# Two-layer hybrid transformer block, one core: three FFN norms folded into the eviction, products of 384 and 386 columns

## What is computed

```python
def rms_norm(x, w):
    return x * lax.rsqrt(jnp.mean(x * x, axis=-1, keepdims=True) + NORM_EPS) * w

def modulate(h, shift, scale):
    return h * (1.0 + scale) + shift

def swiglu(h, w_in, w_out):
    gate, up = jnp.split(h @ w_in, 2, axis=-1)
    return (jax.nn.silu(gate) * up) @ w_out

for layer in range(2):
    h = h + 0.5 * lm[2] * swiglu(modulate(rms_norm(h, norm_w[layer, 0]), lm[0], lm[1]), ffn_w_in[layer, 0], ffn_w_out[layer, 0])
    ...
    h = h + lm[5] * y
    h = h + 0.5 * lm[8] * swiglu(modulate(rms_norm(h, norm_w[layer, 2]), lm[6], lm[7]), ffn_w_in[layer, 1], ffn_w_out[layer, 1])
```

## Time and profile before

| | |
|---|---|
| median of 3 runs | 2738.08 us (2736.44 to 2738.50) |
| the profiled execution, its own time | 2739.12 us |
| its span | 2737.2 us |
| PE (matmul) busy | 2664.7 us, 97% |
| DVE busy | 1521.2 us, 56% |
| ACT busy | 692.3 us, 25% |
| mean granted TensorE clock | 0.992 |
| chain that ended last, by engine | PE 91%, DVE 4%, ACT 2%, issue 1%, POOL 1% |

### The profile page before, as it was taken

How to read it: one execution, slowest core, us unless ns; L and a number is a source line. 1 busy time by engine, 2 the same in 40 slices (tenths; PEclk the granted TensorE clock), 3 DMA queues, 4 the chain that set the end, 5 groups by cost and what they waited for, 6 DMA issues and landing times.

```text
span 2737.2 us, 42267 instructions
## 1 busy us (share of the span) xinstructions
PE 2664.7 (97%) x15515; PEld 2290.5 (84%) x15515; DVE 1521.2 (56%) x2621; ACT 692.3 (25%) x1075; POOL 93.7 (3%) x211
## 2 busy tenths in 40 slices
PE   7999999999999999999999999999999989999998
PEld 4888888888877888888888888888887877888886
DVE  5776477534376477626763677247536465543333
ACT  4111111122256221111111311111113345422222
POOL 0000000000034000000000000000000022000000
PEclk8999999999999999999999999999999999999999
DMA  7877477412200177536762577257422200233332
GB/s 228 198 184 185 113 184 184 125 50 79 54 17 2 54 165 185 146 86 159 184 161 58 123 184 175 71 140 184 126 70 84 69 26 17 81 96 100 91 110 81
DMA packets 485795, 316.98 MB, mean 116 GB/s; under 512 B 30588, under 2 KB 483664, under 8 KB 485712
## 3 DMA queue, kind: packets, MB, share of 16 engines
q1 hardware_dynamic: 485712, 315.88, 45.2%
HBM read 313.73 MB, written 2.10 MB: 115 GB/s over the span
## 4 chain that ended last, share of the span: by engine, by line
PE 91%; DVE 4%; ACT 2%; issue 1%; POOL 1%; DMA 0%; SPq 0%; DVEq 0%; ACTq 0%; POOLq 0%
PE pg L709 79%; PE pg L776 4%; PE p L1047 1%; PE pn L1030 1%; PE pg L986 1%; PE p L724 1%; DVE xlo L1640 1%; DVE tnorm L1632 1%; PE pg L867 1%; ACT whi L1155 0%; DVE wlo L1493 0%; PE pg L991 0%; DVE probT L1847 0%; DVE mx L1854 0%; ACT xhi L1244 0%
## 5 line engine op out<-in xcount | busy, mean ns | idle before, releaser
L709 PE MATMUL pg<-xhi,whi 128*128 128x512 f32 (+1 forms) x2856 | 794.5, 347 | 4.1 <-DVE wlo L1493 4.0
L709 PE MATMUL pg<-xhi,wlo 128*128 128x512 f32 (+1 forms) x2856 | 788.6, 344 | 0.0
L709 PE MATMUL pg<-xlo,whi 128*128 128x512 f32 (+1 forms) x2856 | 787.1, 344 | 0.0
L1155 ACT CAST whi<-raw 128x1024 fp32r<-128x1024 f32 (+1 forms) x288 | 321.8, 1118 | 1060.2 <-PE pg L709 1045.9
L1493 DVE TENSOR_TENSOR wlo<-raw,whi 128x1024 fp32r<-128x1024 f32 (+1 forms) x288 | 377.6, 1311 | 350.5 <-ACT whi L1155 347.8
L709 PEld LDWEIGHTS pg<-xhi,whi 128*128 128x128 f32 x2856 | 451.3, 188 | 72.6 <-DVE wlo L1493 5.9
L709 PEld LDWEIGHTS pg<-xlo,whi 128*128 128x128 f32 x2856 | 450.4, 188 | 69.3
L709 PEld LDWEIGHTS pg<-xhi,wlo 128*128 128x128 f32 x2856 | 450.4, 188 | 68.9
L1577 DVE SCALAR_TENSOR_TENSOR part<-ada,cond,part 128x256 f32<-128x256 f32 x960 | 465.3, 485 | 32.7
L1703 DVE SCALAR_TENSOR_TENSOR h<-pg,gcol,h 128x512 f32 (+1 forms) x118 | 71.4, 639 | 442.3 <-PE pg L709 437.5
L709 PE MATMUL pg<-ahi,whi 128*128 128x512 f32 x1100 | 306.1, 346 | 0.0
(11 more groups left out here) (212 smaller groups left out, 1983.4 us busy)
## 6 DMA issues: line engine op xcount, KB each, us to landing
ada<-in_w_ada SPq DMA_DIRECT2D x512, 256.0 KB, 4.2
raw<-in_ffn_w_in SPq DMA_DIRECT2D x176, 512.0 KB, 3.9
raw<-in_ffn_w_out SPq DMA_DIRECT2D x64, 704.0 KB, 4.5
raw<-in_w_in SPq DMA_DIRECT2D x24, 512.0 KB, 3.8
ada_first<-in_w_ada SPq DMA_DIRECT2D x8, 1024.0 KB, 11.9
raw<-in_w_in SPq DMA_DIRECT2D x16, 256.0 KB, 3.5
raw<-in_w_o SPq DMA_DIRECT2D x16, 256.0 KB, 2.8
raw<-in_w_o SPq DMA_DIRECT2D x32, 128.0 KB, 2.9
```

The costliest lines, as they stand in the source:

```text
L709: last = nc.tensor.matmul(pg[s][:, p0:p1], w[:, s, k], v[:, k, p0:p1], start=(k == 0 and n == 0), stop=(k == kt - 1 and n == 2))
L1155: nc.scalar.copy(whi[:, s, 0:nk], raw[:, s, 0:nk]).then_inc(s_whi[s], 1)
```

## The change

It concerns the norms `m` = 0, 2 and 3 (`POST`), all of them ahead of an FFN over 768 tokens.

- **The operand.** `xhi`/`xlo` hold `h * acol` alone (norm weight and scale), without the root and without the shift. ACT makes `xhi` straight from `h` (`scaled_hi`) and DVE makes `xlo` straight from `h` (`scaled_low`). Two more columns, 768 and 769, hold the shift vectors of the latent and of the context tokens (`shift_columns_hi`, `shift_columns_low`), so rows of `xhi` and `xlo` are 776 floats apart instead of 768.
- **The products** of these phases go over columns 0 to 383 and 384 to 769, that is 384 and 386 columns, one to each bank of `pg[s]`.
- **The eviction.** DVE multiplies unit 0 by `rstd` from PSUM into `gate`, copies its two shift results to `gbias`, and frees PSUM. ACT then takes Silu from `gate` with `gbias` as bias, in two instructions. DVE multiplies unit 1 by `rstd` into `up`, and makes `(up + gbias) * gate` in two more.
- **The norm's order.** The root is taken behind the operands. In norm 3, the operands of `k` 0 to 5 are made ahead of the last pair's eviction (`EARLY_K`); in norm 2 all are made behind it.
- **The opening.** ACT squares the token rows of `xtok` with an accumulator into `ssq`, one number for each token; DVE spreads these on a diagonal, and the same matmul by ones turns it into a row. The eight squares and eight additions over `h` go. DVE copies five of the six transposes, ACT the last. PE's two sums of squares come ahead of the first modulation chunk. ACT loads the table and takes the roots behind the operands of the second chunk.

```diff
+        POST = (0, 2, 3)
+        EARLY_K = {3: KD - 2}
+        def product_parts(i, t):
+            if phases[i][0] in ("in", "win") and phases[i][2] in POST:
+                return [(0, TOK // 2, 0), (TOK // 2, XB, 512)]
+            return [(0, SEQ, 0)] + ([(SEQ, t, SEQ)] if t > SEQ else [])
...
-                parts = [(0, SEQ)] + ([(SEQ, TOK)] if t == TOK else [])
+                parts = product_parts(i, t)
...
-                        if part_ == 0 and (s, k) == (0, 1):
+                        if part_ == 0 and (s, k) == (order[-1] if m in POST else (0, 1)):
                             square_sums(m, 1)
             def opening_pair(i):
-                first_modulation(0)
                 square_sums(0, 0)
                 square_sums(0, 1)
+                first_modulation(0)
                 first_fold(0)
...
-            for tt in range(0, TOK // P, 2):
-                act.wait_ge(s_xT, tt + 1)
...
+            for tt in range(TOK // P):
+                act.wait_ge(s_x[tt // 2], 32)
...
+                nc.scalar.activation(sqjunk[tt % 2][:, :], xtok[:, tt, :], ACT.Square, accum_out=ssq[:, tt:tt + 1]
...
-            for k in range(KD):
-                square(0, k, k % 2, 1)
...
+            def scaled_hi(m, part_, k):
+                nc.scalar.activation(xhi[:, k, p0:p1], h[:, k, p0:p1], ACT.Identity, scale=acol[:, k, v:v + 1]
+                                     ).then_inc(s_xh, 1)
...
+                        if m in POST:
+                            split_hi(nxt, 0, jn)
+                            act.wait_ge(s_free[0], read_value(i, f))
+                            nc.scalar.activation(gate[:, 0:SEQ], gate[:, 0:SEQ], ACT.Silu, bias=gbias[:, 0:1])
+                            nc.scalar.activation(gate[:, SEQ:TOK], gate[:, SEQ:TOK], ACT.Silu, bias=gbias[:, 1:2]
+                                                 ).then_inc(s_gd, 1)
+                            split_hi(nxt, 1, jn)
+                            return
...
+            def scaled_low(m, part_, k):
+                nc.vector.scalar_tensor_tensor(xlo[:, k, p0:p1], h[:, k, p0:p1], acol[:, k, v:v + 1],
+                                               xhi[:, k, p0:p1].bitcast(f32), ALU.mult, ALU.subtract).then_inc(s_xn, 1)
...
+                        if m in POST:
+                            dve.wait_ge(s_unit[0], f + (j0 + 1))
+                            nc.vector.tensor_tensor(halves_of(gate[:, :]), unit_columns(0), halves_of(rstd[:, :]), ALU.mult)
+                            nc.vector.tensor_copy(gbias[:, 0:2], pg[0][:, shift_at]).then_inc(s_free[0], 1)
                         split_lo(nxt, 0, jn)
...
+                        if m in POST:
+                            nc.vector.tensor_copy(gbias[:, 2:4], pg[1][:, shift_at])
+                            nc.vector.tensor_tensor(halves_of(u), unit_columns(1), halves_of(rstd[:, :]), ALU.mult).then_inc(s_free[1], 1)
+                            dve.wait_ge(s_gd, gate_count(m, hf, f))
+                            for v, (p0, p1) in enumerate(((0, SEQ), (SEQ, TOK))):
+                                last = nc.vector.scalar_tensor_tensor(gate[:, p0:p1], u[:, p0:p1],
+                                                                      gbias[:, 2 + v:3 + v], gate[:, p0:p1],
+                                                                      ALU.add, ALU.mult)
```

More of the change, by code:

```diff
@@ L141, in transformer @@
         gate = place("gate", [P, TOK], f32, m0 + TOK * 4)
+        up = place("up", [P, HALF, TOK], f32, start["alo"])
+        gbias = sb("gbias", [P, 4])
+        sqjunk = [place(f"sqjunk{b}", [P, D], f32, at) for b, at in enumerate((m0 + 3 * TOK * 4, m0 + 4096))]
+        ssq = place("ssq", [P, TOK // P], f32, m0 + 3 * TOK * 4 + D * 4)
         xtok = place("xtok", [P, TOK // P, D], f32, start["alo"])
@@ L707, in split_product @@
                     for n, (w, v) in enumerate(((whi, hi), (whi, lo), (wlo, hi))):
-                        for p0, p1 in parts:
-                            last = nc.tensor.matmul(pg[s][:, p0:p1], w[:, s, k], v[:, k, p0:p1],
+                        for p0, p1, c0 in parts:
+                            last = nc.tensor.matmul(pg[s][:, c0:c0 + p1 - p0], w[:, s, k], v[:, k, p0:p1],
                                                     start=(k == 0 and n == 0), stop=(k == kt - 1 and n == 2))
@@ L1440, in _ @@
                     else:
-                        square_part(i, 0, 0)
-                        square_part(i, 0, 1)
+                        nn = next_norm(i)
+                        early = EARLY_K.get(nn, 0)
+                        if early:
+                            act.wait_ge(s_coef, coef_count(nn, 0))
+                            for part_ in range(2):
+                                if part_:
+                                    shift_columns_hi(nn, 0, KD)
+                                for k in range(early):
+                                    scaled_hi(nn, part_, k)
+                        for s in range(2):
+                            square_part(i, 0, s)
+                            if early:
+                                scaled_hi(nn, 0, early + s)
                 else:
@@ L1666, in norm @@
                         read_first(q)
-                        scaled(0, 2 * q)
-                        scaled(1, 2 * q)
-                        low(0, 2 * q)
-                        scaled(0, 2 * q + 1)
-                        low(1, 2 * q)
-                        scaled(1, 2 * q + 1)
+                        scaled_low(0, 0, 2 * q)
+                        shift_columns_low(0, 2 * q, 2 * q + 2)
+                        scaled_low(0, 1, 2 * q)
+                        scaled_low(0, 0, 2 * q + 1)
                         if q == 0:
                             copy_first(1)
-                        low(0, 2 * q + 1)
-                        low(1, 2 * q + 1)
+                        scaled_low(0, 1, 2 * q + 1)
+                    return
+                if m in POST:
+                    if phases[i][0] == "wo":
+                        for k in range(3):
+                            scaled_low(m, 0, k)
+                        add_part(i, 1, 0)
+                        split_lo(i + 1, 0, 0)
+                        scaled_low(m, 0, 3)
+                        sum_part(m, 1, 0)
+                        for k in (4, 5):
+                            scaled_low(m, 0, k)
+                        add_part(i, 1, 1)
+                        split_lo(i + 1, 1, 0)
+                        for k in (6, 7):
+                            scaled_low(m, 0, k)
+                        sum_part(m, 1, 1)
+                        shift_columns_low(m, 0, KD)
+                        for k in range(KD):
+                            scaled_low(m, 1, k)
+                    else:
+                        split_lo(i + 1, 0, 0)
+                        sum_part(m, 1, 0)
+                        add_part(i, 1, 1)
+                        scaled_low(m, 1, KD - 2)
+                        split_lo(i + 1, 1, 0)
+                        sum_part(m, 1, 1)
+                        scaled_low(m, 1, KD - 1)
                     return
@@ L1896, in step @@
                         dve.wait_ge(s_unit[1], f + (j0 + 1))
[L1897 removed]
+                        if m not in POST:
+                            dve.wait_ge(s_free[0], read_value(i, f))
                         col = slice(f, f + 1) if isinstance(f, int) else ds(f, 1)
@@ L1944, in _ @@
                         coefficients(nn)
+                        early = EARLY_K.get(nn, 0)
+                        for part_ in range(2):
+                            if early and part_:
+                                shift_columns_low(nn, 0, KD)
+                            for k in range(early):
+                                scaled_low(nn, part_, k)
                         for s in range(2):
@@ L1947, in _ @@
                             sum_part(nn, 0, s)
-                        add_part(i, 1, 0)
+                            if early:
+                                scaled_low(nn, 0, early + s)
+                        if early or nn not in POST:
+                            add_part(i, 1, 0)
                 else:
```

157 lines of the change are left out of this document (118 added, 39 removed).

## The result

| | before | after |
|---|---|---|
| median, same chip | 2738.29 us (2736.44 to 2741.03) | 2755.98 us (2753.76 to 2758.57) |
| ratio, 95% interval | | 1.0063 [1.0047, 1.0079] |
| the profiled execution, its own time | 2739.12 us | 2758.57 us |

A forecast was written before the change was run, and what follows sets the result against it. PE, busy 97% of the span, was taken to bound the kernel. Opening -4.5, norm 2 -3.5, norm 3 -4.0 and products +2.6 sum to -9.4 us: 2729 us, range 2721 to 2740.

The forecast's parts named there:

- the products' term: FFN products, 3168 couples: two more columns each, 0.83 ns, with the number of matmuls unchanged; +2.6 us.
- The rival of the slower pace: FFN products at the new widths run at the mixing's 355 ns a couple: 19.3 us more, 2748 us; chance 0.09.
- The lower end of the products' term: FFN products: a couple could fall to 770/2.4 + 2 x 8 ns, put at -15 us.
- the sign of being wrong: FFN loop: the prediction is wrong if a pair of units takes over 17.3 us, or PE's fold waits for DVE.
- Opening: Start to the first FFN's loop: earlier products, later third chunk, shorter operand waits and end; -4.5 us, ends -2.8 and -5.5.
- a wait ahead of the third fold: Opening: table load and roots delay the copy of chunk 2 beyond PE's other work; +1.0 us.
- Norm 2: Last pair to the FFN's loop: first product 2 us earlier, a later hole included; -3.5 us, ends -4.8 and -1.0.
- a hole of 1.40 us for 2.0 ahead of slot 1's products: Norm 2: slot 1's weights come late behind ACT's square and operands, so PE waits 2.0 us.
- The half of a low stretch: Norm 2: PE's clock may fall again, costing 1.7 to 3.4 us; half of the smaller was taken.
- Norm 3: Last pair to the FFN's loop: fewer waits, with six of eight operands made ahead; -4.0 us, ends -4.5 and -2.5.
- DVE's step: FFN loop's steady step: added DVE work disappears in a 2.69 us wait, margin 1.1 us; costed at nothing.
- the bound that it might stay low for 5 us of products: Opening's end of -2.8 us: clock at 0.50 rises at 39.6 only, so 5 us of products run at half rate.

The follow-up runs named there:

- the kernel without shift columns: The changed kernel with rows 768 floats apart, the two shift columns left out and products of 384 and 384 columns: 2722.54 us, ratio 0.9937.
- the rows above, of another kernel: The kernel before with the opening's part alone, squares from token rows and roots ahead of chunk 0's copy: 2740.04 us, ratio 0.9994.
- streams alone: Separate kernels that only stream the same matmuls, nothing else running, by row distance, widths, order and entry; 384 + 386 at 776 in the changed layout: 353 to 354 ns a couple.

## Why the prediction was wrong

**The step that failed** is the products' term: "a matmul costs its columns plus some 13.4 ns, whatever its width", hence +2.6 us. It measured 0.30 us a pair, +19.8 us over 66. The formula was fitted to 512 and 256, at a distance of 768, and used for 386 at 776. Half is the distance (16.90 with it alone), the rest two more columns and the split: at 832, where the distance is harmless, 384 + 386 still has 353 ns in every stretch. I had listed the change of row distance, under the rival, but as a matter of the 3168 couples. That the last FFN, with widths untouched, reads the same rows was not in the sum: +5.9.

**The rival of the slower pace** was nearest to what happened: it names the widths, the distance and the tail, and leaves open which counts. That its size fits, 6.1 ns a couple for 6.2, is partly luck: the 6.1 came from 512 + 256 at 768, and the 6.2 are a distance and a split. I gave it 0.09 because three streams fitted a formula. What should have weighed more is that the trace of before already held couples at 355 ns with no hole that I could name, and that its out phases, which I had not looked at one by one, don't all fit the formula. The stretch of 312 couples that holds the first out phase behind norm 2 (start, length, work), before:

```profile
1147.07 110.38 PE pg L709 x624
```

is 353.8 ns a couple, for the 346.8 of the formula. The rival's 2748 was short of 2756 by the last FFN's rows and the out phases' pace.

**Two slips beside it.** The lower end of the products' term does not follow from its working: 770/2.4 + 2 x 8 is 336.8 ns, 10 under the formula's 346.8 before, which is -32 us and not -15. And the sign of being wrong, a pair over 17.3 us, was set too far out: 17.05 was enough to lose 19 us.

**The out phases' pace** was missing too. Looking at six of them, not at one, would have shown two paces, and that 0.2% of the time can move by itself when code around a phase changes.

**What held.** Opening: -4.70 for -4.5; its first product at 34.88 for 34.5, with a wait ahead of the third fold of 0.36 us for 1.0. Norm 2: -4.6 for -3.5, with a hole of 1.40 us for 2.0 ahead of slot 1's products, and the clock did not fall behind it:

```profile
950.00:975.00 25.00, 23.60 (x147) 22.75 (x146) 16.08 (x28) 18.41 (x31) 0.00 (x0) 1.00 0.52 123
```

The half of a low stretch that I had charged was not paid. Norm 3: -3.7 for -4.0. Sum -13.1 for -12.0, and the kernel without shift columns shows them whole: 13.6 us of its 17 under before. DVE's step: nothing, as costed. In the opening the clock was at 0.57 until 36.8 and at 1.00 from there; the bound that it might stay low for 5 us of products was not needed.

**The table load.** In the changed kernel's opening it starts at 41.66 and takes 1.28 us, and the next ACT instruction starts at 42.95, 0.01 us behind its end; the rows above, of another kernel, show the same 0.01. The Trainium skill (ScalarE: Activation LUTs, What ACT_TABLE_LOAD costs) has 1.38 us of drain behind the load. By that rule the opening would have been 1.4 us worse; the trace does not show it, and the measurement decides.

## What to carry to other kernels

Where one engine is busy 97% of the time, price a changed operand's layout (distance of rows, start, width, order of widths) before anything it saves elsewhere: 6 ns on each of 3168 couples outweighed three closed holes. Try a distance of a multiple of 256 bytes for the moving operand's rows first (here 226.7 to 227 ns for 512 columns, 231.8 to 233.0 at all others), and measure a new split in streams alone, entered in several ways, before it goes into the kernel. And compare kernels phase by phase: a phase that nobody edited can change its pace, and an early gain of 4 us went mostly into that.

## What the runs showed of the hardware

- Products of 512 float32 columns (rounded type) took 226.7 to 227 ns at row distances of 768, 832, 896 and 1024 floats, and 231.8 to 233.0 at 770, 772, 776, 784 and 800.
- At 832: 384 columns 173.4 ns, 386 176.6, 400 180.0, 416 188.3. N columns do not take N/2.4 plus one constant: what is left over is 13.3 to 15.8 ns at 384 to 416 columns, and 20.0 at 448 (206.7). The Trainium skill (TensorE: Matmul & The Clock Gate, "Wait — 56ns, not 53.3ns?") has N/2.4 GHz + 2.5 ns, 215.7 ns for 512, between bf16 matmuls issued back to back; with the rounded float32 here the smallest is 226.7.
- A stretch of 512 + 256 at 768 or 832 holds 346.7 or 353.3 ns a couple, chosen as it is entered; 384 + 384 at 768 had only 346.7. 256 + 512 had mostly 353.3 in streams alone, though 346.8 in one, and 346.7 in most phases of a whole kernel.
- **Open:** why the distance counts, and what at the entry picks the pace. The runs show that these set the time, not how. Open too is why PE's clock falls behind one 2.3 us wait in layer 1's attention in some kernels and not in others.
